# Norms of the latent projections placed among the matmuls, value weights released in halves, and another slot order for layer 1's first expert loads

## The chip, the cores and the metric

The kernel runs on one core of one Trainium2 chip. TensorE multiplies, ScalarE (ACT) and VectorE (DVE) work elementwise, GpSimd (POOL) helps with a few elementwise products, and SyncE (SP) issues the DMAs that bring weights from HBM. The engines run side by side and meet only at semaphores. The metric is the device time of one launch in microseconds (us).

## The reference

`reference` runs two blocks in sequence on x (512 tokens x 1024 channels). `first_block` has two layers. Each layer projects both the 512 tokens and 256 context tokens, does two kinds of attention and a short convolution, merges the branches, and then runs an expert layer in which each of 16 experts takes its best tokens. `second_block` is one layer more, with a dilated attention and a latent attention whose input is normalised twice before it is expanded. What matters here of the latter:

```python
proj = xn @ w_in
q_c  = proj[..., IN_A:IN_A + 512]           # four column tiles of 128
kv_c = proj[..., IN_A + 512:IN_A + 768]     # two column tiles
k_pe = proj[..., IN_A + 768:IN_A + 800]
q  = rms_norm(q_c, q_norm) @ w_uq           # 8 heads x 96, rotary on the last 32
kv = rms_norm(kv_c, kv_norm) @ w_ukv        # 8 heads x (64 key + 64 value)
```

## The kernel before, in words

Activations lie transposed in SBUF, channels on partitions and tokens along the row. The order of all work is written out by hand, one function for each engine and stage (`pe_second`, `act_second`, `dve_second` for the second block), and each engine runs its own list strictly in that order. A `Signal` counts finished steps; `up` raises it, `at` names the count to wait for.

**Dense products in three passes.** float32 accuracy comes from splitting each operand into a high and a low part in a reduced format. For a weight piece of up to 128 x 1024 values that SP has loaded into one of six half slots of `ring`, ScalarE copies the high part to WH (`act_high`, L538), VectorE subtracts to get the low part WL (`dve_low`, L547), and TensorE multiplies (`pe_linear3`, L574). WH and WL hold two pieces, so piece q may be split only when TensorE has finished with piece q-2, and `act_high` waits for the `dn` signal of the *unit* (one call of a product) to which that piece belongs. All units have one piece, except the value units ("v" of each layer, and three of them in the second block), which have two of 512 rows each. `pe_values3` (L593) multiplies them with tokens as the output rows, steps k=0..3 from the first piece and k=4..7 from the second.

**PSUM.** Four tiles go round in a fixed queue: `bank.take(key, freed)` gives the next tile and notes what frees it for the one after.

**Latent projections.** In the second block, after the dilated attention (AD), six units ("c",0) to ("c",5) give q_c and kv_c, a unit "pe" gives k_pe. ScalarE copies each result out (L2295). Then `act_norm` squares the tiles (L694), TensorE sums the squares over partitions with a matrix of ones (L711), ScalarE makes the reciprocal root by Ln and Exp (L729, L731; two table loads), and VectorE multiplies (`dve_norm`, L2383). This is done for "nq" (4 tiles), then for "nkv" (2 tiles). `act_aside` (L602) and `dve_aside` (L607) split the four normalised q tiles into high and low parts. Then come eight heads of queries, ("uq", h//2), two heads for each weight piece (`pe_aside`, L622), each followed by its rotary (`pe_rope` L873, `act_rope_in` L880, POOL L894, DVE L901 and L910), then keys and values from KV by plain float32 products (L2213, L2220), and the latent attention (AM).

**Expert loads.** Layer 1's 192 loads of 1 MB go through SP in the order in which TensorE uses them (`sp_experts`, L2559). There are 12 slots: 0 to 2 are `ring`, 3 to 6 lie in memory freed once the layer's norm sum is done (`p_n`, L723), 7 to 11 lie in the arena and are used once. Of the latter, 7 to 9 are free when h2 is transposed (L1494) and 10 and 11 when the mask is transposed (L1504). Load n < 12 goes to slot n; after that the seven slots 0 to 6 go round, and a load waits until the one before it in its slot has been multiplied (L1899 for gate and up, L1934 for down):

```python
s = self.n if self.n < len(self.aps) else (self.n - len(self.aps)) % self.turn
```

The functions that the diff touches follow.

Of the kernel before, what the change touches and what calls it, by code (L numbers as in the profile page):

```python
# [14 lines left out]
NX = 512  # L15
# [192 lines left out]
class Slots:  # L208

    def __init__(self, aps, sems, once=0):
        self.aps, self.sems, self.count, self.n, self.turn = aps, sems, [0] * len(sems), 0, len(aps) - once

    def add(self, srcs, many, kind, what):
        s = self.n if self.n < len(self.aps) else (self.n - len(self.aps)) % self.turn
        self.n += 1
        self.count[s] += 16 * len(srcs)
        return s, srcs, many, kind, what, (self.sems[s], self.count[s])
# [16 lines left out]
def build(nc, I, cst, cmask, crope, at, out):  # L236
    ctx = ExitStack()
    with ctx:
# [94 lines left out]

        MD, ME, MO = [None] * 3, [None] * 2, [None] * 2
        ONCE = (14336, 16384, 22528, 18432, 20480)
        fulls = [ring[:, i * SLOT:(i + 1) * SLOT] for i in range(KEPT)]
        early = []
        for l in (0, 1):
# [9 lines left out]
            MO[l].stack.close()  # L348
            under.close()
        MD[2] = dense_memory(2)  # L350
        ES = [Slots(fulls + early[0] + MO[0].slots, s_w), Slots(fulls + early[1] + [AR(a, SLOT) for a in ONCE], s_w[:7] + s_o, len(ONCE))]

        identb = MB[:, MI:MI + 128]
        ident = K("ident")
# [169 lines left out]
        def unit_of_split(X, q):  # L524
            return next(u for u, x in enumerate(X.units) if x[0] <= q < x[1])

        def act_high(e, X, u):
            if u >= len(X.units):  # L530
                return
            m = MD[int(X.key[1])]
            for q, (s, srcs, many, kind, what, arrived) in split_pieces(X, u):
                e.wait_ge(*arrived)
                if q > 1:
                    e.wait_ge(*dn.at(X.key, unit_of_split(X, q - 2)))
                o = 1024 * (q % 2)
                e.activation(m.WH[:, o:o + many], halves.aps[s][:, 0:many], ACT.Copy).then_inc(*hi.up(X.key, q))  # L538

# [37 lines left out]
        def pe_values3(e, X, name, chunks, low, key, *freed):  # L577
            u = X.unit[name]
            m = MD[int(X.key[1])]
            wh, wl = halves_of(X, u)  # L580
            bufs = []
            for n in range(0, chunks, 4):
                ps, when = bank.take((key, n // 4), freed[n // 4])
                bufs.append(ps)
                for w in when:
                    e.wait_ge(*w)
            e.wait_ge(*lo.at(X.key, X.units[u][1] - 1))
            for k in range(KD):
                if low:
                    e.wait_ge(*low(k))  # L590
                for c in range(chunks):
                    for p, (h, w) in enumerate(((m.XH, wh), (m.XL, wh), (m.XH, wl))):
                        i = e.matmul(bufs[c // 4][:, 256 * (c % 4):256 * (c % 4) + 256], h[:, k, c * 128:(c + 1) * 128], w[:, k, :],  # L593
                                     start=k == 0 and p == 0 and c % 2 == 0, stop=k == 7 and p == 2, skip_group_check=True)
            i.then_inc(*dn.up(X.key, u))

        def aside(t, c):
# [1580 lines left out]
        def pe_second(e):  # L2178
# [8 lines left out]
            e.wait_ge(*c_ev.at("x2", "v", 2))  # L2187
            e.wait_ge(*d_o.at("ra", 11))
            pe_attention(e, AD)
            for c in range(6):  # L2190
                pe_linear3(e, X2, ("c", c), 128, NX, ("x2", "c", c), c_ev.at("x2", "c", c))
            pe_linear3(e, X2, "pe", 96, NX, ("rp", "r", 0), c_ev.at("rp", "y", 0))
            pe_rope(e, "rp", 0, NX, 96, ROT[:, 128:256], False)
            for stage, kn in (("nq", 4), ("nkv", 2)):
                pe_norm_take(e, stage)
                for k in range(kn):
                    pe_square(e, stage, k, kn, NX, sqr[k % 2])
            for h in range(8):
                pe_aside(e, X2, ("uq", h // 2), "qc", 96, 4, 96 * (h % 2), h % 2, ("ru", "r", h), c_ev.at("ru", "y", h))
                if h:  # L2200
                    pe_rope(e, "ru", h - 1, NX, 96, ROT[:, 128:256], False)
            pe_rope(e, "ru", 7, NX, 96, ROT[:, 128:256], False)
            p = [X2.plain["ukv", k] for k in (0, 1)]
            for k in (0, 1):
# [68 lines left out]
        def act_norm(e, stage, src, kn, n):  # L2273
            for k in range(kn):
                act_square(e, stage, k, src(k), NX, sqr)
            act_rstd(e, stage, kn, NX, n)

        def act_second(e):
            act_split_gain(e, "gain")
# [8 lines left out]
            e.wait_ge(*d_o.at("ra", 11))  # L2288
            act_attention(e, AD)
            for c in range(6):  # L2290
                act_high(e, X2, X2.unit["c", c] + 1)
                e.wait_ge(*dn.at("x2", X2.unit["c", c]))
                if c == 0:
                    e.wait_ge(*a_pv.at("ad", len(AD.groups) - 1))
                e.activation((QC[:, c, :] if c < 4 else KV[:, c - 4, :]), bank.of["x2", "c", c][:, 0:NX], ACT.Copy).then_inc(*c_ev.up("x2", "c", c))  # L2295
            act_high(e, X2, X2.unit["pe"] + 1)
            act_rope_in(e, "rp", 0, NX, 96, 1.0, dn.at("x2", X2.unit["pe"]), False)
            e.wait_ge(*d_o.at("rp", 0))
            act_norm(e, "nq", lambda k: QC[:, k, :], 4, 512)
            e.wait_ge(*d_an.at("nq", 3))  # L2300
            act_norm(e, "nkv", lambda k: KV[:, k, :], 2, 256)
            e.wait_ge(*d_an.at("nkv", 1))
            for c in range(4):
                act_aside(e, X2, "qc", QC, c)
            for h in range(8):
                if h % 2 == 0:
                    act_high(e, X2, X2.unit["uq", h // 2] + 1)
                act_rope_in(e, "ru", h, NX, 96, 1.0, uq(h), False)
            for h in range(8):
                e.wait_ge(*p_br.at("x2", "kh", h))  # L2310
                e.activation(KH[0:64, h, :], bank.of["x2", "kh", h][0:64, 0:NX], ACT.Copy).then_inc(*c_ev.up("x2", "kh", h))
                e.activation(KH[64:96, h, :], KP[64:96, 0, :], ACT.Copy).then_inc(*c_ev.up("x2", "kp", h))
# [90 lines left out]
        def dve_second(e):  # L2403
# [11 lines left out]
            dve_attention(e, AD)  # L2415
            for c in range(6):
                dve_low(e, X2, X2.unit["c", c] + 1)
            dve_low(e, X2, X2.unit["pe"] + 1)
            dve_rope(e, "rp", 0, NX, 96, rope[:, 3], KP[64:96, 0, :], 64, False)
            dve_norm(e, "nq", QC, 4, 64)  # L2420
            dve_norm(e, "nkv", KV, 2, 68)
            for c in range(4):
                dve_aside(e, X2, "qc", QC, c)
            for h in range(8):
# [225 lines left out]
```

## Time and profile before

| | us |
|---|---|
| median of 3 runs (3680.44 to 3684.14) | 3680.85 |
| profiled execution, its own time | 3679.47 |
| its span, first to last instruction | 3677.7 |
| TensorE busy | 3401.4 (92% of the span) |
| VectorE busy | 1248.5 (34%) |
| ScalarE busy | 1025.4 (28%) |
| GpSimd busy | 186.8 (5%) |
| bytes read from HBM | 595.56 MB, 163 GB/s over the span |
| mean granted TensorE clock | 0.974 |

Times inside the profile count from the first instruction. The rows below give a start and a duration, the engine, the line of the kernel, what is written and read, and in brackets how long the engine had been idle and who ended that. A granted clock of 1.00 is 2.4 GHz and 0.50 is 1.2 GHz; values between are mixtures over a stretch.

### The profile page before, as it was taken

How to read it: one execution, taken by the hardware profiler on the slowest of the kernel's cores; microseconds unless marked ns; L12 is line 12 of the kernel's file. 1: busy time of each engine (PE TensorE's matmuls, PEld its weight loads, DVE VectorE, ACT ScalarE, POOL GpSimd, SP SyncE). 2: the span in 40 equal slices, each digit the busy share in tenths (PEclk: the TensorE clock that was granted, in tenths of full speed). 3: DMA queues.
4: the chain of work that ended last, by engine and by line, in shares of the span. 5: the costliest groups of instructions: out<-in, count | busy, mean ns of one | idle time of the engine just before them, and what ended most of it. 6: DMA issues, size and time to landing. Idle time of an engine off the chain costs nothing.

```text
span 3677.7 us, 48715 instructions
## 1 busy us (share of the span) xinstructions
PE 3401.4 (92%) x21634; PEld 2284.5 (62%) x21634; DVE 1248.5 (34%) x1750; ACT 1025.4 (28%) x1641; POOL 186.8 (5%) x121
## 2 busy tenths in 40 slices
PE   6999999999899999999999979988888989989997
PEld 5787677887534344377668864332247656858886
DVE  3225642323411011144663351111142434453333
ACT  3623532223210000055452231000031344342222
POOL 0100000111100000000000120000001010110000
PEclk9999999999899999999999989999989989989998
DMA  6440014223499989812003348999952111323331
GB/s 223 132 132 24 1 58 115 63 64 128 167 374 354 384 348 358 309 46 81 18 7 98 92 154 313 409 409 409 409 188 69 39 35 41 91 58 97 92 98 46
DMA packets 359985, 600.82 MB, mean 163 GB/s; under 512 B 48770, under 2 KB 242656, under 8 KB 359648
## 3 DMA queue, kind: packets, MB, share of 16 engines
q1 hardware_dynamic: 357024, 596.62, 45.8%
q8 instruction: 171, 2.80, 0.3%
q10 hardware_dynamic: 2752, 1.09, 0.1%
q14 instruction: 38, 0.31, 0.0%
HBM read 595.56 MB, written 2.10 MB: 163 GB/s over the span
## 4 chain that ended last, share of the span: by engine, by line
PE 84%; DMA 6%; DVE 6%; ACT 3%; issue 1%; ACTq 0%; POOL 0%; POOLq 0%; SPq 0%; DVEq 0%
PE ps L574 32%; PE ps L1904 6%; PE ps L2256 5%; PE ps L1060 4%; PE ps L622 4%; PE ps L1899 3%; PE ps L1149 3%; PE ps L1907 3%; PE ps L1938 3%; PE ps L1110 3%; PE ps L1324 3%; DMA ring<-in_w_e_down 3%; DMA ring<-in_w_e_up 2%; PE ps L593 2%; PE ps L1934 2%; PE ps L1551 2%
## 5 line engine op out<-in xcount | busy, mean ns | idle before, releaser
L574 PE MATMUL ps<-xh,wh 128*128 128x512 f32 x1912 | 650.9, 378 | 35.8 <-DVE xl L2118 11.4
L574 PE MATMUL ps<-xl,wh 128*128 128x512 f32 x1912 | 632.9, 369 | 0.0
L574 PE MATMUL ps<-xh,wl 128*128 128x512 f32 x1912 | 632.7, 369 | 0.0
L547 DVE TENSOR_TENSOR wl<-ring,wh 128x1024 fp32r<-128x1024 f32 (+1 forms) x259 | 333.8, 1290 | 615.2 <-ACT wh L538 613.9
L574 PEld LDWEIGHTS ps<-xh,wh 128*128 128x128 f32 x1912 | 332.7, 190 | 123.1 <-issue 39.3
L538 ACT ACTIVATE wh<-ring 128x1024 fp32r<-128x1024 f32 (+1 forms) x259 | 271.7, 1050 | 457.2 <-PE ps L574 168.1
L574 PEld LDWEIGHTS ps<-xl,wh 128*128 128x128 f32 x1912 | 332.9, 191 | 63.5 <-issue 4.3
L574 PEld LDWEIGHTS ps<-xh,wl 128*128 128x128 f32 x1912 | 331.5, 190 | 62.0
L1904 PE MATMUL ps<-ring,arena 128*32 128x512 f32 x2048 | 267.2, 593 | 1.0 <-DVE arena L1686 1.0
L1899 PE MATMUL ps<-ring,arena 128*64 128x512 f32 x984 | 226.9, 599 | 17.9 <-DMA ring<-in_w_e_gate 9.0
L1899 PEld LDWEIGHTS ps<-ring,arena 128*64 128x64 f32 x984 | 66.4, 136 | 154.7 <-issue 101.4
L1907 PEld LDWEIGHTS ps<-ring,arena 128*32 128x32 f32 x2048 | 66.7, 110 | 153.0 <-issue 153.0
L1907 PE MATMUL ps<-ring,arena 128*32 128x256 f32 x2048 | 157.4, 379 | 0.0
L1071 DVE TENSOR_REDUCE sm<-ps 128x2 f32<-128x1536 f32 (+3 forms) x96 | 142.3, 1482 | 43.6 <-PE ps L1060 43.5
L1060 PE MATMUL ps<-arena 64*128 64x256 f32 (+3 forms) x800 | 150.2, 449 | 2.6 <-DVE arena L1020 1.8
L1110 PE MATMUL ps<-consts,tmp 128*128 128x128 f32 x832 | 127.3, 285 | 20.0 <-DVE arena L1166 12.0
L1089 ACT ACTIVATE tmp<-ps,sm 128x768 f32<-128x768 f32 (+3 forms) x176 | 132.7, 762 | 46.3 <-DVE sm L1074 38.8
L1934 PE MATMUL ps<-ring,arena 128*64 128x512 f32 x512 | 114.6, 595 | 31.5 <-DMA ring<-in_w_e_down 23.9
L1110 PEld LDWEIGHTS ps<-consts,tmp 128*128 128x128 f32 x832 | 88.8, 141 | 58.4 <-issue 21.6
L2059 DVE SCALAR_TENSOR_TENSOR y<-ps,gate,y 128x1024 fp32r<-128x1024 f32 x16 | 20.5, 1284 | 307.0 <-ACT y L1994 307.0
L1938 PE MATMUL ps<-ring,hbuf 128*32 128x512 f32 x1024 | 121.8, 592 | 0.8 <-DVE hbuf L2051 0.8
L1149 PE MATMUL ps<-arena 128*64 128x256 f32 (+1 forms) x896 | 99.6, 368 | 14.6 <-DVE arena L1133 14.6
(271 smaller groups left out, 4376.7 us busy)
## 6 DMA issues: line engine op xcount, KB each, us to landing
ring<-in_w_e_down SPq DMA_DIRECT2D x128, 1024.0 KB, 8.2
ring<-in_w_e_gate SPq DMA_DIRECT2D x126, 1024.0 KB, 9.0
ring<-in_w_e_up SPq DMA_DIRECT2D x125, 1024.0 KB, 9.1
ring<-in_w_in SPq DMA_DIRECT2D x116, 512.0 KB, 3.9
ring<-in_w_ada SPq DMA_DIRECT2D x96, 512.0 KB, 4.7
ring<-in_w_ff SPq DMA_DIRECT2D x64, 512.0 KB, 3.9
ring<-in_w_out SPq DMA_DIRECT2D x24, 512.0 KB, 3.7
ring<-in_w_in SPq DMA_DIRECT2D x40, 256.0 KB, 3.8
```

What stands on the lines that cost most here:

```text
L538: e.activation(m.WH[:, o:o + many], halves.aps[s][:, 0:many], ACT.Copy).then_inc(*hi.up(X.key, q))
L547: e.tensor_tensor(m.WL[:, o:o + many], halves.aps[s][:, 0:many], m.WH[:, o:o + many].bitcast(F32), ALU.subtract).then_inc(*lo.up(X.key, q))
L574: i = e.matmul(ps[0:M, a:b], w[:, k, 0:M], h[:, k, a:b], start=k == 0 and p == 0, stop=k == 7 and p == 2)
L1060: x = e.matmul(ps[:, col:col + k.shape[-1]], q, k, start=first, stop=last, skip_group_check=True)
L1110: x = e.transpose(ps[:, 128 * c:128 * c + 128], src[:, u, 128 * b:128 * b + 128], ident)
L1149: e.matmul(ps[r0:r0 + 64, q0:q1], v, pt, start=x == 0, stop=x == len(pv) - 1, skip_group_check=True)
L1899: i = e.matmul(pa[64 * h:64 * h + 64, 512 * w:512 * w + 512], rows_of(1, kk, x, 0, 64), W[:, k, 512 * h:512 * h + 512], start=kk == 0, sto ...
L1904: e.matmul(pa[64 * h + g:64 * h + g + 32, 512 * w:512 * w + 512], rows_of(0, kk, x, g, g + 32), W[:, k, 512 * h:512 * h + 512], start=kk = ...
L1907: i = e.matmul(pb[32 * q:32 * q + 32, 256 * w:256 * w + 256], rows_of(0, kk, x, 64, 96), W[:, k, 256 * q:256 * q + 256], start=kk == 0 and ...
L1934: i = e.matmul(ps[64 * x:64 * x + 64, 512 * h:512 * h + 512], HT2[p % 2][:, x, k % 4, k // 4, :], w, start=k == 0, stop=k == 7)
L1938: e.matmul(ps[64 * x + g:64 * x + g + 32, 512 * h:512 * h + 512], HX[:, k, 64 * x + g:64 * x + g + 32], w, start=k == 0, stop=k == 7, skip ...
L2256: i = e.matmul(accs(d), w[:, 0, d * 128:(d + 1) * 128], h[:, f % 8, 0:NX], start=f == 0 and p == 0, stop=f == 31 and p == 2)
```

## The change

It has three parts.

**Value units in halves.** `pe_values3` waits for the low part of its first piece before k=0 and of its second before k=4, where it waited for the second before k=0. It raises a second signal, `dn(..., "half")`, after k=3, and `act_high` waits for that instead of the whole unit when the piece it overwrites is the first of two (`multiplied`).

**Norms among the projections.** TensorE sums the "nq" squares after unit ("c",4), and the "nkv" squares after the first rotary of the heads. ScalarE squares the q tiles after copying out ("c",3), makes the root after ("c",4), splits the q tiles before the rotary of "pe", and makes the "nkv" root after head 1. VectorE follows. The squares get buffers of their own (`sqm`).

**Slot order.** The first twelve loads of layer 1 go to slots 0, 1, 2, 7, 3, 8, 4, 9, 5, 10, 6, 11.

```diff
+            return dn.at(X.key, u, "half") if q < X.units[u][1] - 1 else dn.at(X.key, u)
...
-                    e.wait_ge(*dn.at(X.key, unit_of_split(X, q - 2)))
+                    e.wait_ge(*multiplied(X, q - 2))
...
-            e.wait_ge(*lo.at(X.key, X.units[u][1] - 1))
+            first = X.units[u][0]
             for k in range(KD):
+                if k % 4 == 0:
+                    e.wait_ge(*lo.at(X.key, first + k // 4))
...
+                if k == 3:
+                    i.then_inc(*dn.up(X.key, u, "half"))
...
-        s = self.n if self.n < len(self.aps) else (self.n - len(self.aps)) % self.turn
+        s = self.first[self.n] if self.n < len(self.aps) else (self.n - len(self.aps)) % self.turn
...
+        FIRST = (0, 1, 2, 7, 3, 8, 4, 9, 5, 10, 6, 11)
...
 pe_second
+            def norm(stage, kn):
+                pe_norm_take(e, stage)
+                for k in range(kn):
+                    pe_square(e, stage, k, kn, NX, sqm[k % 2])
             for c in range(6):
                 pe_linear3(e, X2, ("c", c), 128, NX, ("x2", "c", c), c_ev.at("x2", "c", c))
+                if c == 4:
+                    norm("nq", 4)
...
-            for stage, kn in (("nq", 4), ("nkv", 2)):
-                pe_norm_take(e, stage)
-                for k in range(kn):
-                    pe_square(e, stage, k, kn, NX, sqr[k % 2])
...
+                if h == 1:
+                    norm("nkv", 2)
...
 act_second
+                if c == 3:
+                    act_high(e, X2, X2.unit["c", 4] + 1)
+                    for k in range(4):
+                        e.wait_ge(*c_ev.at("x2", "c", k))
+                        act_square(e, "nq", k, QC[:, k, :], NX, sqm)
+                if c == 4:
+                    act_high(e, X2, X2.unit["c", 5] + 1)
+                    act_rstd(e, "nq", 4, NX, 512)
             act_high(e, X2, X2.unit["pe"] + 1)
+            for c in range(4):
+                e.wait_ge(*d_an.at("nq", c))
+                act_aside(e, X2, "qc", QC, c)
+            for k in range(2):
+                e.wait_ge(*c_ev.at("x2", "c", 4 + k))
+                act_square(e, "nkv", k, KV[:, k, :], NX, sqm)
             act_rope_in(e, "rp", 0, NX, 96, 1.0, dn.at("x2", X2.unit["pe"]), False)
             e.wait_ge(*d_o.at("rp", 0))
-            act_norm(e, "nq", lambda k: QC[:, k, :], 4, 512)
-            e.wait_ge(*d_an.at("nq", 3))
-            act_norm(e, "nkv", lambda k: KV[:, k, :], 2, 256)
-            e.wait_ge(*d_an.at("nkv", 1))
...
                 act_rope_in(e, "ru", h, NX, 96, 1.0, uq(h), False)
+                if h == 1:
+                    act_rstd(e, "nkv", 2, NX, 256)
...
 dve_second
+            dve_norm(e, "nq", QC, 4, 64)
             dve_low(e, X2, X2.unit["pe"] + 1)
...
+                if h == 3:
+                    dve_norm(e, "nkv", KV, 2, 68)
```

## Rows read from the trace of the kernel before

**Rows 1.** The page: the chain that ended last by engine, and a costly group.

```profile
PE 84%; DMA 6%; DVE 6%; ACT 3%; issue 1%; ACTq 0%; POOL 0%; POOLq 0%; SPq 0%; DVEq 0%
...
L538 ACT ACTIVATE wh<-ring 128x1024 fp32r<-128x1024 f32 (+1 forms) x259 | 271.7, 1050 | 457.2 <-PE ps L574 168.1
```

**Rows 2.** Chain in order of time, value units: start us, us, what.

```profile
54.55 18.83 PE ps L593 x144
75.83 8.59 PE ps L574 x48
...
1589.27 19.38 PE ps L593 x144
1611.19 18.18 PE ps L574 x96
...
2805.38 11.76 PE ps L593 x96
2820.72 11.78 PE ps L593 x96
2836.18 13.16 PE ps L593 x96
```

**Rows 3.** TensorE timeline: the last rotary ahead of the value units.

```profile
2803.63 1.13 PE L873 MATMUL ps<-tmp 128*128 128x512 f32 x2 [0.83 <-ACT tmp L880]
```

**Rows 4.** Chain in order of time, latent projections and heads.

```profile
2899.03 38.44 PE ps L574 x168
...
2963.11 8.59 PE ps L622 x48
2972.57 2.80 PE ps L622 x24
```

**Rows 5.** Stretches: length, busy by engine, granted clock, DMA share, GB/s.

```profile
2837.00:2850.00 13.00, 12.33 (x94) 12.12 (x93) 0.00 (x0) 0.57 (x1) 0.00 (x0) 0.91 0.24 67
2938.00:2963.00 25.00, 10.21 (x14) 3.37 (x14) 6.24 (x10) 12.79 (x18) 1.26 (x1) 0.71 0.00 0
2963.00:2971.00 8.00, 7.88 (x44) 7.92 (x45) 2.64 (x4) 2.13 (x4) 0.00 (x0) 0.62 0.26 68
2971.00:2996.00 25.00, 25.00 (x167) 20.11 (x166) 11.81 (x16) 6.57 (x10) 8.93 (x7) 1.00 0.17 43
```

**Rows 6.** ScalarE timeline, latent norms.

```profile
2945.63 0.63 ACT L694 ACTIVATE tmp<-arena 128x512 f32<-128x512 f32 x1 [0.81 <-PE ps L711]
...
2961.61 2.19 ACT L602 ACTIVATE xh<-arena 128x512 fp32r<-128x512 f32 x4 [1.48 <-DVE arena L2383]
2963.71 0.82 ACT L538 ACTIVATE wh<-ring 128x768 fp32r<-128x768 f32 x1
```

**Rows 7.** VectorE timeline, latent norms.

```profile
2940.68 0.68 DVE L910 TENSOR_TENSOR arena<-tmp 32x512 f32<-32x512 f32 x1 [0.66 <-POOL tmp L894]
2950.23 2.74 DVE L2383 SCALAR_TENSOR_TENSOR arena<-arena,PT,tmp 128x512 f32<-128x512 f32 x4 [8.87 <-ACT tmp L731]
...
2962.28 2.50 DVE L607 TENSOR_TENSOR xl<-arena,xh 128x512 fp32r<-128x512 f32 x4 [0.70 <-ACT xh L602]
```

**Rows 8.** TensorE timeline: one sum of squares in layer 1, and the rotary of "pe".

```profile
2168.12 1.02 PE L720 MATMUL ps<-tmp,ones 128*128 128x512 f32 x2
...
2938.23 1.07 PE L873 MATMUL ps<-tmp 96*96 96x512 f32 x2 [0.78 <-ACT tmp L880]
```

**Rows 9.** SP timeline, layer 1: issue of loads 3, 7, 18 and 19.

```profile
2170.94 0.37 SPq L2559 DMA_DIRECT2D ring<-in_w_e_up  x1
...
2190.18 0.37 SPq L2559 DMA_DIRECT2D arena<-in_w_e_up  x1
...
2231.14 0.37 SPq L2559 DMA_DIRECT2D ring<-in_w_e_gate  x1
...
2244.03 0.37 SPq L2559 DMA_DIRECT2D ring<-in_w_e_up  x1
```

**Rows 10.** DMA, 2236 to 2256 us, forty slices of 0.5 us.

```profile
GB/s 410 410 172 115 57 25 0 0 0 0 0 0 0 0 0 0 0 0 33 156 434 393 418 426 410 377 410 434 410 410 418 418 442 410 352 287 360 385 352 303
```

More of the change, by code:

```diff
@@ L208, with __init__ @@
 class Slots:
-    def __init__(self, aps, sems, once=0):
+    def __init__(self, aps, sems, once=0, first=None):
         self.aps, self.sems, self.count, self.n, self.turn = aps, sems, [0] * len(sems), 0, len(aps) - once
+        self.first = first or range(len(aps))
     def add(self, srcs, many, kind, what):
-        s = self.n if self.n < len(self.aps) else (self.n - len(self.aps)) % self.turn
+        s = self.first[self.n] if self.n < len(self.aps) else (self.n - len(self.aps)) % self.turn
         self.n += 1
@@ L350, in build @@
         MD[2] = dense_memory(2)
-        ES = [Slots(fulls + early[0] + MO[0].slots, s_w), Slots(fulls + early[1] + [AR(a, SLOT) for a in ONCE], s_w[:7] + s_o, len(ONCE))]
+        ES = [Slots(fulls + early[0] + MO[0].slots, s_w), Slots(fulls + early[1] + [AR(a, SLOT) for a in ONCE], s_w[:7] + s_o, len(ONCE), FIRST)]
         identb = MB[:, MI:MI + 128]
@@ L525, in unit_of_split, with multiplied @@
             return next(u for u, x in enumerate(X.units) if x[0] <= q < x[1])
+        def multiplied(X, q):
+            u = unit_of_split(X, q)
+            return dn.at(X.key, u, "half") if q < X.units[u][1] - 1 else dn.at(X.key, u)
         def act_high(e, X, u):
@@ L2271, in accs @@
             return bank.of["acc", (d // 2 + 1) % 4][:, 512 * (d % 2):512 * (d % 2) + 512]
[L2273 to L2276, printed above, removed]
+        sqm = [tmp[:, 4096:4608], tmp[:, 4608:5120]]
         def act_second(e):
@@ L2290, in act_second @@
             for c in range(6):
-                act_high(e, X2, X2.unit["c", c] + 1)
+                if c < 4:
+                    act_high(e, X2, X2.unit["c", c] + 1)
                 e.wait_ge(*dn.at("x2", X2.unit["c", c]))
@@ L2295, in act_second @@
                 e.activation((QC[:, c, :] if c < 4 else KV[:, c - 4, :]), bank.of["x2", "c", c][:, 0:NX], ACT.Copy).then_inc(*c_ev.up("x2", "c", c))
-            act_high(e, X2, X2.unit["pe"] + 1)
+                if c == 3:
[6 more added lines that the diff above has]
+                    act_rstd(e, "nq", 4, NX, 512)
+            act_high(e, X2, X2.unit["pe"] + 1)
+            for c in range(4):
[4 more added lines that the diff above has]
+                act_square(e, "nkv", k, KV[:, k, :], NX, sqm)
             act_rope_in(e, "rp", 0, NX, 96, 1.0, dn.at("x2", X2.unit["pe"]), False)
             e.wait_ge(*d_o.at("rp", 0))
-            act_norm(e, "nq", lambda k: QC[:, k, :], 4, 512)
-            e.wait_ge(*d_an.at("nq", 3))
-            act_norm(e, "nkv", lambda k: KV[:, k, :], 2, 256)
-            e.wait_ge(*d_an.at("nkv", 1))
-            for c in range(4):
-                act_aside(e, X2, "qc", QC, c)
             for h in range(8):
@@ L2417, in dve_second @@
                 dve_low(e, X2, X2.unit["c", c] + 1)
+            dve_norm(e, "nq", QC, 4, 64)
             dve_low(e, X2, X2.unit["pe"] + 1)
-            dve_rope(e, "rp", 0, NX, 96, rope[:, 3], KP[64:96, 0, :], 64, False)
-            dve_norm(e, "nq", QC, 4, 64)
-            dve_norm(e, "nkv", KV, 2, 68)
             for c in range(4):
                 dve_aside(e, X2, "qc", QC, c)
+            dve_rope(e, "rp", 0, NX, 96, rope[:, 3], KP[64:96, 0, :], 64, False)
             for h in range(8):
```

## The prediction, made before the changed kernel was run

> **What bounds the kernel now.** I read the page first, then the chain in order of time, then each engine's timeline around the three places that the diff touches, then stretches with their granted clock. TensorE carries 84% of the chain that ended last [rows 1]; in the dense stages the whole path is its own list, and a microsecond without a multiplication there is a microsecond of the run. The exception is layer 1's expert stage, where loads arrive at some 410 GB/s without a break [rows 10]. Each edit is therefore priced as a hole in TensorE's list, or as bytes moved earlier.
>
> The holes in the chain: after each value unit TensorE stands still until the next unit's pieces are split [rows 2], and between the end of "pe" and the first head lie 25.6 us (2899.03 + 38.44 = 2937.5 to 2963.11) with little but the norms [rows 4]. After long holes the granted clock is low: 0.71 and 0.62 behind the norms, 0.91 in the third value unit, against 1.00 once the heads run [rows 5].
>
> **Value units in halves.** ScalarE can split the piece behind a value unit at its middle. The mid-point lies some 5.9 us (layers: 9.5 us) ahead of the unit's end, and splitting one piece takes 1.05 us on ScalarE [rows 1] and a little more on VectorE, so it is ready. The second piece of the next unit still waits for the end, but is wanted only after four steps, 5.9 us later. So each hole closes:
> - Layer 0: 75.83 - (54.55 + 18.83) = 2.45 us [rows 2].
> - Layer 1: 1611.19 - (1589.27 + 19.38) = 2.54 us [rows 2]. The two units behind it take 18.18 us, against 2 x 8.59 = 17.2 in layer 0: 1.0 more at the lower clock, which I count as regained.
> - Second block: ahead of the first unit TensorE waits for the low part of the second piece, from the end of the last rotary (2803.63 + 1.13 = 2804.76) to 2805.38, 0.6 us [rows 2, 3]. Between the units 2820.72 - 2817.14 = 3.58 and 2836.18 - 2832.50 = 3.68. The third unit takes 13.16, not 11.77: 1.4 at the lower clock. Behind it ScalarE now splits the next piece (1.05) before it copies the values out, and attention waits for that copy; with the split done at the half, 1.0 is gained.
>
> Both layers' gains pass on: behind them come stages led by TensorE, and layer 1's load stream starts only when TensorE has multiplied load 12, so it moves with it. Sum: 2.45 + 3.54 + 10.26 = 16.3 us. The added waits stand in front of work whose inputs are long there, and no instruction is added. The start of the layers' value units stays: what they wait for there is the split of the activations.
>
> **Norms among the projections.** One dense unit takes 38.44 / 7 = 5.49 us [rows 4], so ("c",4) ends at 2899.03 + 5 x 5.49 = 2926.5, and the first head starts 36.6 us later. Count the new list from that end (time 0). *TensorE:* four sums of squares at the 1.02 us of layer 1's [rows 8], to 4.1; ("c",5) to 9.6; "pe" to 15.1; the rotary starts 0.8 later as now and takes 1.0 [rows 8], to 16.9; then head 0. *ScalarE* did two squares ahead, does the other two between TensorE's sums by about 2.8 (0.63 each [rows 6]), copies ("c",4) out to 3.4, splits "pe" to 4.3 (0.82), and makes the root. A root takes, from the last square's end (2946.26) to VectorE's first product at 2950.23 [rows 6, 7], 4.0 us with both table loads: 8.3. It copies ("c",5) at its end, to 10.2, splits the first head piece to 11.0, and the q tiles to 13.2 (2.19 [rows 6]). *VectorE* normalises from 8.3 to 11.1 (2.74), and finishes the low parts of the tiles at about 14.5 (2.50 and one weight piece [rows 7]). TensorE wants them at 16.9: 2.4 us of slack. The hole shrinks by 36.6 - 16.9 = 19.7.
>
> Queued behind the new waits: behind ScalarE's third square stand the copy of ("c",4) and the split of "pe", wanted only at 9.6; behind the rotary of "pe" (done 3.5 us after its end at most, [rows 7, 8]: 2940.68 + 0.68 against 2937.5 is 3.9) stand the next split and head 0's copy, wanted by TensorE only after head 1, 7.5 us after "pe". At head 1 the "nkv" root holds ScalarE for some 5 us, and behind it are the split of the third head piece, wanted two heads later (7 us), and head 2's copy, wanted 8 us later. VectorE's two more products (1.4) lie between rotaries that leave it idle more than half the time. I find nobody waiting. The two "nkv" sums now cost TensorE 2 x 1.02 = 2.0 between heads; they were in the old hole.
>
> The heads: the first two take 8.59, later ones 2.80 to 2.87 each [rows 4], so 2.9 us were lost to the low clock. With no hole over 1 us before them I count that as gained. Sum: 19.7 - 2.0 + 2.9 = 20.6 us. The squares and the weighted sum themselves are unchanged in number.
>
> Rows show both levels: 0.62 granted over the first heads, 1.00 after [rows 5]. The Trainium skill, "TensorE: Matmul & The Clock Gate", Part 1, says that the clock is halved after idling and released by sustained activity; by that rule all three clock terms (5.3 us) come back. Without it the sum would be 31.6 instead of 36.9. The switch of table costs 1.3 us in the trace (the root starts that long after the square). "ScalarE: Activation LUTs", What ACT_TABLE_LOAD costs, in the Trainium skill, gives 2.66 us for a switch, with a drain behind the load; two switches would be 2.8 us longer and would use up the slack of 2.4. The measured root has no room for such drains, so I keep the row.
>
> **Slot order.** Load 3 now waits for h2 instead of the norm sum: 2190.18 instead of 2170.94, and loads 4 to 6 stand behind it in SP's queue [rows 9]. They still land long before their turn: load 6 was multiplied when load 18 could go out, at 2231.14, and six loads at 410 GB/s take 15.4 us from 2190. Loads 15 to 18 then wait for loads 4, 6, 8 and 10 instead of 3 to 6, so the stream is spread out, the last leaving when load 10 is done, about 2239.7 if loads 6 to 12 are evenly spaced, instead of 2231.14. But load 19 waits for load 12 before and after (2244.03). Nineteen loads have gone out at that time either way, and from there the stream runs without a break to the end of the stage. The trace shows the DMA engines idle from 2239 to 2245 [rows 10]: the new order fills that hole with bytes which it takes from earlier holes. Bounds: a gain of 6 us if it filled it with new bytes, a loss of 19.2 if the late start weighed in full. By the count of loads I take 0.
>
> **Sum.** 16.3 + 20.6 + 0 = 36.9 us. The profiled execution took 3679.47 (span 3677.7) and would take 3642.6; the median of the runs, 3680.85, lies 1.4 above it: **3644**.
>
> **Rivals.**
> - *The low clock stays.* The holes close, but the three clock terms are not regained: 3649. For it, 0.91 was granted over a stretch in which TensorE was busy 12.33 of 13 us [rows 5]; against it, 1.00 in the heads.
> - *A queue stalls.* The root in the heads, or the late split of the q tiles, holds up TensorE. The slack is 2.4 us and the root 4: a price of 2 to 6 us, 3646 to 3650. By the page's price for table switches it would be near the lower end, about 3645.
> - *The slot order matters.* It gains the 6 us of the idle stretch, 3638, or loses 19, 3663. The count of loads speaks against both.
> - *Slower.* Layer 1's loads lose their overlap: if the new order left one load in flight at a time through the stage, each would add at least the 1.2 us from issue (2244.03) to the first bytes (2245.2) [rows 9, 10]. This decides from about 31 such loads on (36.9 / 1.2); all 173 left would cost 208 us, 3852 in all. Against it: from load 12 on the seven slots go round as before, and only seven loads change what they wait for.
> - *No change.* The holes move instead of closing, ScalarE being so late in all of them: 3681. Its busy 12.8 of 25 us in the norm stretch [rows 5] speaks against it.
>
> **How the numbers follow.** Forecast 0.62, low clock 0.12, a stall 0.12, slot gain 0.04, slot loss 0.05, no change 0.02, slower by overlap lost 0.03. The range 3637 to 3652 takes in the forecast, the low clock, the stalls and the slot gain, 0.90, less what their own sizes may miss. A measurement of this kernel can tell about 0.2% (7 us) from no change: faster 0.95, same 0.02, slower 0.03.
>
> **What would show it.** Right: the chain has no hole over 1 us behind a value unit; the third takes 11.8; the first head starts about 17 us after ("c",4) ends, and two heads take 5.7; load 19 leaves when load 12 is done, and layer 1's stage is as long as before. Wrong: TensorE waiting for `xl` or `wl` at the heads, for ScalarE's squares behind ("c",4), or for a load in layer 1's first experts.

## The result, and the profile after

| | before | after |
|---|---|---|
| median of the runs, us | 3681.49 (4 runs, 3680.44 to 3684.14) | 3639.64 (4 runs, 3637.78 to 3642.18) |
| ratio, 95% interval | | 0.9886 [0.9869, 0.9903] |
| span of the profiled execution, us | 3677.7 | 3640.3 |
| mean granted TensorE clock | 0.974 | 0.977 |

The change saves 41.9 us (1.14%); 36.9 were forecast. The two profiled spans lie only 37.4 us apart, as the forecast had it: the profiled execution of after, at 3642.18 us, was the slowest of its four, 2.5 us above their median, and the one of before, at 3679.47, lies 2.0 us below its own. These 4.5 us of the gain are the difference between executions and cannot be found between these two profiles.

The page of after, the chain by engine, answers to [rows 1]:

```profile
span 3640.3 us, 48719 instructions
...
PE 85%; DMA 6%; DVE 5%; ACT 3%; issue 1%; ACTq 0%; POOL 0%; POOLq 0%; SPq 0%; DVEq 0%
```

The chain of after in order of time (start us, us, what); L581 is `pe_linear3` now, L602 `pe_values3`, L633 `pe_aside`, L722 `pe_square`:

```profile
55.08 20.12 PE ps L602 x144
75.20 8.48 PE ps L581 x48
...
1589.18 19.46 PE ps L602 x144
1608.64 16.97 PE ps L581 x96
...
2802.56 34.56 PE ps L602 x288
...
2885.79 27.44 PE ps L581 x120
2913.22 3.62 PE ps L722 x8
2916.85 11.02 PE ps L581 x48
...
2929.70 5.67 PE ps L633 x48
...
2937.95 2.79 PE ps L633 x24
```

Read it against [rows 2, 4]. Every value unit ends where the next link starts: 1589.18 + 19.46 = 1608.64, with no hole. In the second block the three value units have become one link, 34.56 us for 288 matmuls, where three links of 11.76, 11.78 and 13.16 us lay with 3.6 and 3.7 us between them; in after that link starts where the rotary ahead of it ends (2801.43 + 1.13 = 2802.56), so the hole of 0.6 us there is closed too. Behind ("c",4) the chain now goes to the sums of squares (3.62), then ("c",5) and "pe" (11.02), and the first head starts 43.9 us after ("c",0), where it took 64.1, and 16.5 us after ("c",4) ends (2913.22 to 2929.70; 16.9 were forecast). Two heads take 5.67 us, which is two times a later head.

Stretches at the start of the values of layer 0, before and after, and over the first heads of after (length, busy time by engine, granted clock, DMA share, GB/s). The last answers to the 0.62 of [rows 5]:

```profile
54.00:60.00 6.00, 5.45 (x34) 5.48 (x35) 5.89 (x13) 2.65 (x6) 0.00 (x0) 0.71 0.65 154
...
54.00:60.00 6.00, 4.92 (x23) 4.95 (x24) 5.89 (x11) 2.88 (x6) 0.00 (x0) 0.50 0.71 197
...
2928.00:2936.00 8.00, 7.37 (x52) 6.43 (x53) 2.33 (x3) 2.40 (x4) 1.30 (x1) 1.00 0.14 31
```

The heads ran at full clock. Layer 0's value unit began at half clock in both executions; in this one the clock stayed low for longer (0.50 up to 60 us, where before had 0.71), and the unit took 20.12 us instead of 18.83. The hole behind it is closed all the same (55.08 + 20.12 = 75.20).

ScalarE and VectorE of after around the norm, which answer to [rows 6, 7]: the two table loads with Ln and Exp, and the split of the q tiles.

```profile
2916.90 1.28 ACT L740 ACT_TABLE_LOAD   x1
2918.20 0.69 ACT L740 ACTIVATE tmp<-ps,eps 128x512 f32<-128x512 f32 x1
2918.90 1.28 ACT L742 ACT_TABLE_LOAD   x1
2920.20 0.63 ACT L742 ACTIVATE tmp<-tmp 128x512 f32<-128x512 f32 x1
```

```profile
2924.57 2.49 DVE L618 TENSOR_TENSOR xl<-arena,xh 128x512 fp32r<-128x512 f32 x4
```

The last low part is done at 2924.57 + 2.49 = 2927.06, and the first head's first matmul is recorded at 2929.13 while its link in the chain starts at 2929.70: a slack of 2.1 to 2.6 us around the forecast 2.4. Ahead of that, TensorE and its sums in after's timeline answer to [rows 8]:

```profile
2913.06 3.78 PE L722 MATMUL ps<-tmp,ones 128*128 128x512 f32 x8
...
2928.63 1.07 PE L884 MATMUL ps<-tmp 96*96 96x512 f32 x2 [0.77 <-ACT tmp L891]
```

SP of after issues loads 3, 18 and 19 at these times ([rows 9] had 2170.94, 2231.14, 2244.03):

```profile
2186.80 0.37 SPq L2584 DMA_DIRECT2D arena<-in_w_e_up  x1
...
2235.94 0.37 SPq L2584 DMA_DIRECT2D ring<-in_w_e_gate  x1
2240.66 0.37 SPq L2584 DMA_DIRECT2D ring<-in_w_e_up  x1
```

Load 3 goes out later and the stream is spread, as forecast. The first expert matmul stands at 2210.8 in after and at 2214.2 before, and load 19 leaves 29.9 us behind it in both (2240.66 - 2210.8 and 2244.03 - 2214.2).

### The profile page after: what moved, and what is told of

Same layout as the page of the kernel before. It is cut to its first block, busy times and chain, and to the rows that moved or that the text cites. A ratio compares the mean times of both kernels' runs of the same rounds, so it can differ in the third digit from the quotient of the medians.

```text
span 3640.3 us, 48719 instructions
## 1 busy us (share of the span) xinstructions
PE 3396.2 (93%) x21630; PEld 2280.0 (63%) x21634; DVE 1246.9 (34%) x1750; ACT 1025.2 (28%) x1641; POOL 187.7 (5%) x121
## 3 DMA queue, kind: packets, MB, share of 16 engines
q1 hardware_dynamic: 357024, 596.62, 46.3%
## 4 chain that ended last, share of the span: by engine, by line
PE 85%; DMA 6%; DVE 5%; ACT 3%; issue 1%; ACTq 0%; POOL 0%; POOLq 0%; SPq 0%; DVEq 0%
PE ps L581 32%; PE ps L1915 6%; PE ps L2272 5%; PE ps L1071 4%; PE ps L1910 4%; PE ps L633 3%; PE ps L1160 3%; PE ps L1918 3%; PE ps L1949 3%; PE ps L1121 3%; PE ps L1335 3%; DMA ring<-in_w_e_up 3%; DMA ring<-in_w_e_down 2%; PE ps L602 2%; PE ps L1945 2%; PE ps L1840 2%
## 5 line engine op out<-in xcount | busy, mean ns | idle before, releaser
L581 PE MATMUL ps<-xh,wh 128*128 128x512 f32 x1912 | 648.0, 377 | 32.6 <-DVE xl L2129 13.8
L581 PE MATMUL ps<-xl,wh 128*128 128x512 f32 x1912 | 632.2, 369 | 0.0
L581 PE MATMUL ps<-xh,wl 128*128 128x512 f32 x1912 | 631.9, 369 | 0.0
L581 PEld LDWEIGHTS ps<-xh,wh 128*128 128x128 f32 x1912 | 330.8, 189 | 120.1 <-issue 37.8
L581 PEld LDWEIGHTS ps<-xl,wh 128*128 128x128 f32 x1912 | 331.1, 190 | 63.3 <-issue 4.5
L581 PEld LDWEIGHTS ps<-xh,wl 128*128 128x128 f32 x1912 | 330.9, 190 | 62.4
L1121 PE MATMUL ps<-consts,tmp 128*128 128x128 f32 x832 | 128.6, 287 | 19.6 <-DVE arena L1177 12.0
```

The lines of the kernel that those rows point to most:

```text
L581: i = e.matmul(ps[0:M, a:b], w[:, k, 0:M], h[:, k, a:b], start=k == 0 and p == 0, stop=k == 7 and p == 2)
L1121: x = e.transpose(ps[:, 128 * c:128 * c + 128], src[:, u, 128 * b:128 * b + 128], ident)
```

## The experiments

Beside each result stands the time of the kernel before, measured together with it, and the ratio with its 95% interval. Each kernel was profiled once.

### One part at a time

`e1_values` keeps only the value units in halves: `multiplied`, the waits by piece and the "half" signal.

```diff
             for k in range(KD):
+                if k % 4 == 0:
+                    e.wait_ge(*lo.at(X.key, first + k // 4))
```

> Only the value units in halves; norms and slot order as before. My theory: the three places give 2.5 + 3.5 + 10.3 = 16.3 us, so about 3665. Rival one (the lower clock behind the holes is not caused by them): 13.9 us, the third value unit still takes over 13. Rival two (the layers' share is absorbed before the expert stages): only the second block's 10.3 us, 3671. The profile decides between them: the start of layer 1's first expert, and the length of the third value unit in the second block (11.8 by my theory).

Measured: 3662.72 us against 3681.33, ratio 0.9944 [0.9931, 0.9956], so -18.6. In its chain the three value units of the second block are one link of 34.56 us, three times 11.5, so the third is back at full speed. Layer 1's first expert starts at 2206.9 instead of 2214.2, 7.3 us earlier, of which 1.0 is an earlier start of layer 0's values. The layers' gain is passed on and not absorbed.

```profile
2797.26 34.56 PE ps L600 x288
```

`e2_norms` keeps only the norms among the projections (the hunks of `pe_second`, `act_second` and `dve_second`).

> Only the norms among the projections; value units and slot order as before. My theory: 20.6 us, about 3661; the first head starts 17 us after the unit (c,4) ends, and the first two heads take 5.7 us. Rival (clock not regained): 17.7 us, the first two heads take 8.6. Rival (a queue stalls): a hole in TensorE's list inside the heads, 2 to 6 us less.

Measured: 3660.14 against 3681.33, ratio 0.994 [0.9928, 0.9953], so -21.2. Its chain has what this part leaves alone, the unit behind layer 0's values and the second block's second value unit, and its own two heads:

```profile
76.66 10.28 PE ps L574 x48
...
2823.22 13.27 PE ps L593 x96
...
2947.04 5.67 PE ps L622 x48
```

The second value unit takes 13.27 us here and took 11.78 in [rows 2], and the first unit behind layer 0's values takes 10.28 instead of 8.59. No edit touches them, and the holes ahead of them are the old ones. The granted clock over the second value unit, in before and then in `e2_norms` (length, busy time by engine, clock, DMA share, GB/s), tells the two apart:

```profile
2820.70:2832.50 11.80, 11.77 (x96) 11.56 (x96) 0.00 (x0) 0.00 (x0) 0.00 (x0) 1.00 0.32 90
...
2823.20:2836.50 13.30, 13.26 (x96) 13.06 (x96) 0.00 (x0) 0.00 (x0) 0.00 (x0) 0.87 0.30 79
```

The same five places in all the profiles that still have some of the old holes (us; a dash where the kernel has closed or filled the hole):

| | unit behind layer 0's values | second value unit, second block | its first value unit to ("c",0) | first two heads | last product |
|---|---|---|---|---|---|
| before | 8.59 | 11.78 | 93.65 | 8.59 | 175.99 |
| `e3_slots` | 8.59 | 13.27 | 96.75 | 8.61 | 175.94 |
| `e8_seven_slots` | 10.16 | 13.27 | 95.21 | 7.83 | 174.37 |
| `e5_busy_hole` | 10.16 | 13.27 | 95.22 | - | 174.36 |
| `e2_norms` | 10.28 | 13.27 | 95.22 | - | 174.38 |
| `e6_second_only` | 8.59 | - | - | 7.33 | 174.34 |
| `e1_values` | - | - | - | 7.74 | 174.37 |

The price of a hole in clock thus varies from execution to execution. The profile of before was cheap in the first three columns and dear in the last two.

`e3_slots` keeps only the slot order.

```diff
-        s = self.n if self.n < len(self.aps) else (self.n - len(self.aps)) % self.turn
+        s = self.first[self.n] if self.n < len(self.aps) else (self.n - len(self.aps)) % self.turn
```

> Only the other slot order for layer 1's first twelve loads. My theory: 0 us, 3681, since load 19 waits for load 12 either way; layer 1's expert stage from first to last multiplication is as long as before (468.5 to 471 us). Rival (it explains what the whole change gained beyond my 36.9 us): a gain of 3 to 6 us, load 19 leaving earlier after the first expert's start than before. Rival (the late start weighs): a loss of 1 to 19 us.

Measured: 3683.33 against 3681.33, ratio 1.0002 [0.9993, 1.0011]. The view by source line gives the first and last time of the gate and up matmuls (L1899, L1901) and of the down matmuls (L1934, L1936). Before:

```profile
L1899 PE MATMUL ps<-ring,arena x984: 592/592/644, 2214.2 to 2673.4; 128*64 128x512 f32 x197
L1934 PE MATMUL ps<-ring,arena x512: 592/592/643, 2270.9 to 2696.0; 128*64 128x512 f32 x171
```

`e3_slots`:

```profile
L1901 PE MATMUL ps<-ring,arena x984: 592/592/644, 2214.6 to 2674.7; 128*64 128x512 f32 x197
L1936 PE MATMUL ps<-ring,arena x512: 592/592/644, 2271.3 to 2697.4; 128*64 128x512 f32 x171
```

The stage takes 2696.0 - 2214.2 = 481.8 us before and 2697.4 - 2214.6 = 482.8 with the new order: nothing gained. (The 468.5 to 471 us of the expectation end at the start of the last down product, 2682.66 before.) In all twelve profiles that have the twelve slots, with either order, the stage takes 481.8 to 483.3 us.

`e4_no_slots` is the whole change without the slot order.

```diff
-        ES = [Slots(fulls + early[0] + MO[0].slots, s_w), Slots(fulls + early[1] + [AR(a, SLOT) for a in ONCE], s_w[:7] + s_o, len(ONCE), FIRST)]
+        ES = [Slots(fulls + early[0] + MO[0].slots, s_w), Slots(fulls + early[1] + [AR(a, SLOT) for a in ONCE], s_w[:7] + s_o, len(ONCE))]
```

> The whole change without the slot order. My theory: the same time as the whole change, 3640 within 2 us, and the sum of the two parts alone. Rival (slot order gains 3 to 6 us): 3643 to 3646.

Measured: 3639.51 against 3681.33, ratio 0.9883 [0.9869, 0.9896], and again 3639.51, 0.9883 [0.9866, 0.9899], when it ran once more (`e4_again`) beside later kernels. After has 0.9886. The order of the slots is worth nothing that can be measured, and the parts add up: 18.6 + 21.2 = 39.8 of 41.9 by the medians.

> The whole change without the slot order once more, to stand beside the two kernels below. 3638 to 3641.

### Is it idling that costs the clock?

`e5_busy_hole` is the kernel before, with useless matmuls in the norm hole. They read parts of WH and XH that nobody writes then, and their result is never read. Every sum and every wait of the norms stays; one wait is added ahead, for the low part of the first head piece.

```diff
+            e.wait_ge(*lo.at("x2", X2.units[X2.unit["uq", 0]][0]))
             for stage, kn in (("nq", 4), ("nkv", 2)):
                 pe_norm_take(e, stage)
+                idle(bank.of["norm", stage], 8 if stage == "nq" else 32)
...
+            if name == ("uq", 0) and o == 0:
+                for _ in range(28):
+                    e.matmul(ps[:, 0:256], m.WH[:, 1024:1152], m.XH[:, 0, 0:256], start=True, stop=True)
```

> The kernel before, with 8, 32 and 28 matmuls of no use (128 x 256, into banks that the next product overwrites) in the three parts of the norm hole in which TensorE waits. They end before the work that it waits for arrives. My theory (idling lowered the clock behind the hole): the hole is as long as before, but the first two heads take 5.7 instead of 8.6 us, so the run is 2 to 3 us shorter although TensorE does more. Rival (the lower clock there has another cause): 8.6 us as before.

TensorE of `e5_busy_hole`, two groups of the added matmuls, its chain from ("c",0) to the first heads, and the stretch of these heads:

```profile
2955.28 4.39 PE L2199 MATMUL ps<-xh,wh 128*128 128x256 f32 x32
...
2963.43 3.91 PE L620 MATMUL ps<-xh,wh 128*128 128x256 f32 x28
```

```profile
2907.38 38.45 PE ps L574 x168
...
2969.55 5.90 PE ps L625 x48
...
2969.50:2975.50 6.00, 5.95 (x49) 5.91 (x50) 2.67 (x4) 2.17 (x5) 0.00 (x0) 1.00 0.35 87
```

With a hole that is still there in the chain (62.2 us from ("c",0) to the first head, 64.1 before) the two heads take 5.90 us at a granted 1.00. The five profiles with an idle hole have 7.33 to 8.61, so this one lies outside what the same hole gives by chance. The low clock over the heads comes from what TensorE did in the hole, and not from the heads' own work. The total, 3681.15 in a single run, says nothing about it, since the first expert of layer 1 stood 5.6 us later than in the profile of before, through stages that no edit touches.

`e7_sums_late` is the whole change with the "nq" sums one unit later, which opens a hole again.

```diff
-                if c == 4:
+                if c == 5:
                     norm("nq", 4)
```

> The whole change, but TensorE makes the nq sums after the unit (c,5) instead of (c,4); ScalarE and VectorE keep their lists. My accounting: ScalarE now stands at the third square until (c,5) ends, the split of pe behind it comes 1.5 us too late for TensorE, and the split q tiles 1.9 us too late for the first head; the stretch from the start of (c,0) to the first head is 3.4 us longer than the 43.9 of the whole change, 47.3. Rival (the slack of 2.4 us was larger than I counted): below 45.

Its chain, ("c",0) to ("c",5) and the first heads:

```profile
2884.30 32.88 PE ps L581 x144
...
2930.95 7.22 PE ps L633 x48
```

From ("c",0) to the first head it is 46.65 us, against 43.9 in after, where 47.3 was expected. TensorE now waits for the root's chain ahead of the rotary of "pe":

```profile
2921.97 0.44 PE L581 MATMUL ps<-xh,wh 128*96 128x512 f32 x1 [1.18 <-DVE wl L554]
...
2929.88 1.07 PE L884 MATMUL ps<-tmp 96*96 96x512 f32 x2 [2.14 <-ACT tmp L891]
```

Behind holes of 1.18 and 2.14 us the two heads take 7.22 us, 1.5 more than in after. Its single run took 3645.08 us, 5.4 more than after's median. The two units that the change puts between the sums and the rotary just cover the root; one is too few.

### Where the halves gain

`e6_second_only` is `e1_values` with the halves in the second block alone.

```diff
+            return dn.at(X.key, u, "half") if q < X.units[u][1] - 1 and X.key == "x2" else dn.at(X.key, u)
...
+                    e.wait_ge(*lo.at(X.key, first + (k // 4 if X.key == "x2" else 1)))
```

> Value units in halves in the second block only; layers 0 and 1, norms and slots as before. My theory: the second block's share of 10.3 us, about 3671, which leaves the layers 6 to 8 us of the 18.6 that the part gave alone. Rival (the layers' share is absorbed before the expert stages): 3663 to 3665, the same as with all three places.

Measured: 3667.53 against 3681.37, ratio 0.9966 [0.9954, 0.9978], so -13.8, where 10.3 were forecast. The three value units are one link again:

```profile
2805.17 34.56 PE ps L600 x288
```

The two layers' share by the medians is the rest, 18.6 - 13.8 = 4.8 us. The six runs of this kernel lie between 3664.3 and 3674.3, and its interval reaches from 8.1 to 16.9 us saved, so these two numbers are known to a few microseconds only. The traces divide the gain otherwise. From the start of layer 0's values to its first expert the six kernels with the old hole take 944.5 to 949.5 us (mean 946.2), and the five with the halves and an unchanged start 942.3 to 944.7 (943.2). From the start of layer 1's values to its first expert it is 624.9 to 625.9 (625.4) and 621.4 to 622.5 (621.9). That makes 6.5 us for the two layers, where 6.0 were forecast.

### What the extra slots do

`e8_seven_slots` is the kernel before without its five slots of one use, so that load 7 already waits for a matmul.

```diff
-        ES = [Slots(fulls + early[0] + MO[0].slots, s_w), Slots(fulls + early[1] + [AR(a, SLOT) for a in ONCE], s_w[:7] + s_o, len(ONCE))]
+        ES = [Slots(fulls + early[0] + MO[0].slots, s_w), Slots(fulls + early[1], s_w[:7])]
```

> The kernel before without its five single-use slots in layer 1: seven slots go round from the start. My theory (what counts is when load 12 is done, since load 19 waits for it with twelve slots or with seven): load 19 again leaves when load 12 is done; the DMA engines then still have some 4 us of earlier loads to carry, less than the 6 us for which they stood idle; so 0 to 3 us slower, 3681 to 3684. Rival (each single-use slot saves the time of its 1 MB in the stream, 2.56 us): 12.8 us slower, 3694.

Measured: 3684.82 against 3681.37, ratio 1.0008 [0.9999, 1.0017], so +3.4; the interval just takes in no change at all. SP's issue of load 19, and the stage's first and last matmuls:

```profile
2243.65 0.37 SPq L2559 DMA_DIRECT2D ring<-in_w_e_up  x1
```

```profile
L1899 PE MATMUL ps<-ring,arena x1024: 592/592/669, 2213.8 to 2677.3; 128*64 128x512 f32 x171
...
L1934 PE MATMUL ps<-ring,arena x512: 592/592/1061, 2270.5 to 2700.0; 128*64 128x512 f32 x171
```

The DMA rate of the same kernel from 2200 to 2280 us, forty slices of 2 us:

```profile
GB/s 0 0 0 0 0 0 0 8 123 414 350 356 412 385 379 412 354 397 408 420 410 412 412 410 410 410 410 410 410 410 410 410 410 410 410 408 414 408 408 410
```

Five megabytes fewer are in place, which at 410 GB/s would be 12.8 us; the stage takes 2700.0 - 2213.8 = 486.2 us, 2.9 to 4.4 more than the 481.8 to 483.3 of all profiles with twelve slots. The stream flows from 2216 on without a break, and load 19 leaves at 2243.65 instead of 2244.03. So most of the time that the five loads would have saved was never there. Before, the DMA engines finish early and stand idle from 2239 to 2245 [rows 10]; without the slots they work through that time.

### Further holes

The chain of `e4_no_slots` in its second run still has holes which the same two means close. `e9_further` moves the rotary of "pe" behind head 0, puts head 1's weight piece ahead of the wait for it, and splits layer 0's second value piece between the activation tiles instead of behind them.

```diff
# act_split_mod, dve_split_mod
+                if l == 0 and k == 1:
+                    act_high(e, X, 0, slice(1, 2))
...
+                if l == 0 and k == 2:
+                    dve_low(e, X, 0, slice(1, 2))
...
# act_second
+            act_high(e, X2, X2.unit["uq", 0] + 1)
             e.wait_ge(*d_o.at("rp", 0))
```

> The whole change without the slot order, and two small holes more: TensorE turns pe only behind the first head (the rotary's input then is long there; 0.8 to 1.0 us), and in layer 0 the second value piece is split behind the second and third tile of activations instead of ahead of them, so that the values start 2.3 us earlier and end 2.1 us earlier. About 3 us less than the kernel beside it, 3636 to 3637. Rival (VectorE is what layer 0's values wait for at the end, and it does the same work): 1 us less only.

Measured: 3637.82 against 3681.91, ratio 0.9879 [0.9864, 0.9893], 1.7 us less than `e4_again`, measured together with it. The start of layer 0's values in the chain of `e4_again`, then of `e9_further`, and ScalarE's split of the second value piece in each:

```profile
54.39 19.82 PE ps L602 x144
...
52.69 19.84 PE ps L602 x144
```

```profile
48.75 1.06 ACT L545 ACTIVATE wh<-ring 128x1024 fp32r<-128x1024 f32 x1 [0.67 <-DMA ring<-in_w_in]
...
52.15 1.04 ACT L545 ACTIVATE wh<-ring 128x1024 fp32r<-128x1024 f32 x1
```

The first piece is split at the same time in both (47.03 and 47.06). In `e4_again` the activation tiles stand behind the second, which waits for its DMA; in `e9_further` they don't. So 1.7 us come from the start of layer 0's values, where 2.3 were expected. The rotary gave its part too: from ("c",0) to the third head `e9_further` takes 0.85 us less (51.35 and 52.20). The two chains differ by 2.5 us at these places, the medians by 1.7, and the intervals overlap, so the total alone would not tell the kernels apart.

`e10_tail` adds this: the second product of the feed-forward layer at the end waits for the last tile of the first to be activated and split. The first three tiles it needs are written into a free part of XH and XL while the first product still runs.

```diff
+                moving = aside(h, f) if f < 3 else h[:, f % 8, 0:NX]
```

> The kernel above, and the first three tiles of the feed-forward's second product split into columns of XH and XL that the first product does not read, so that TensorE does not stand still for 2.2 us between the two. 2.2 us less than the kernel above where the clock did not fall behind that hole, 3.8 where it did (the products took 174.4 or 176.0 us): 3633 to 3634.

The chain of `e4_again` ahead of that product, then of `e10_tail`:

```profile
3427.03 0.61 ACT arena L2378
...
3429.23 10.90 PE ps L2272 x47
```

```profile
3421.24 0.61 ACT arena L2393
...
3422.20 17.93 PE ps L2278 x78
```

One link on ScalarE and a short issue stand where ScalarE, VectorE and VectorE had followed each other; the hole shrinks from 2.2 to 1.0 us, and not to nothing as expected. Measured: 3635.57 against 3681.91, ratio 0.9875 [0.986, 0.989]. This kernel has the lowest median here, 46.3 us below before. Against `e4_again` it is 3.9 us lower (four runs each, 3633.68 to 3638.42 and 3636.24 to 3641.29, which still overlap). Its step beyond `e9_further` is 2.2 us by the medians, the number expected, but the chain shows 1.2 of it; the rest is not shown to be the edit's.

## Why the prediction was right

The forecast was 3644 us, the result 3639.64, within the range. Its steps, in order:

| term | forecast | by the medians | by the stages of all traces |
|---|---|---|---|
| value halves, second block | 10.3 | 13.8 (`e6_second_only`; interval 8.1 to 16.9) | 12.6 |
| value halves, two layers | 6.0 | 4.8 (`e1_values` less `e6_second_only`) | 6.5 |
| norms among the projections | 20.6 | 21.2 (`e2_norms`; interval 17.3 to 26.5) | 20.7 |
| slot order | 0 | 0 (`e3_slots`, `e4_no_slots`) | 0 |
| all | 36.9 | 41.9 (interval 35.7 to 48.2) | 39.8 |

The last column takes means over the profiles with and without each part. For the second block they are 95.2 us (the five numbers of the table above) and 83.2 from the first value unit to ("c",0), and 0.6 for the hole ahead of it. For the norms they are 72.8 from ("c",0) to the third head (73.54, 73.64, 72.54, 72.24 and 72.28 in before, `e3_slots`, `e8_seven_slots`, `e1_values` and `e6_second_only`) and 52.2.

**Value units in halves.** The mechanism held at every unit: 1608.64, 75.20 and the single link of 34.56 us. From the first value unit of the second block to ("c",0) before's profile has 93.65 us, after's 83.2, and `e1_values`, `e4_no_slots` and `e6_second_only` have 83.2 too: 10.4 less, where the forecast for this stretch was 9.7 (10.3 without the 0.6 ahead of it). But the other four profiles that leave this part alone have 95.2 to 96.8, and against the mean of the five the halves gain 12.0. In the layers the hole of layer 1 closed as counted (21.92 us from the start of its values to the next unit, now 19.46), and the two units behind it fell from 18.18 to 16.97. In layer 0 the gain shows only in part in after's profile, because there the clock stayed at 0.50 for longer in the values, which began 0.5 us later.

**The step that was mis-sized** is the clock term: I counted 5.3 us over three places, all from [rows 2, 4], one execution. The other traces show that this execution did not stand for the rest. It had no lowered clock in the second value unit (11.78 us, elsewhere 13.27) nor behind layer 0's values (8.59, in three of six 10.2), so I counted nothing at either; and it had the dearest heads but one (8.59 us, elsewhere 7.33 to 8.61, so 2.9 was near the top of 1.7 to 2.9). Most of what was missing lies in the second block's value units, 12.6 by the traces against 10.3; the layers add 0.5, and in the norms the errors cancel. The last product's 1.6 us, in before and in `e3_slots`, is not an effect of the change, since `e2_norms` has the same hole of 2.2 us ahead of it and 174.38 us. The granted clock over its first 8 us, in before and then in `e2_norms`:

```profile
3467.00:3475.00 8.00, 8.00 (x28) 6.43 (x29) 2.73 (x4) 2.01 (x3) 0.00 (x0) 0.79 0.22 68
...
3450.00:3458.00 8.00, 7.84 (x35) 6.50 (x36) 3.86 (x5) 3.18 (x5) 0.00 (x0) 1.00 0.23 68
```

The traces so account for 39.8 us, 2.9 of the error of 5.0. The remaining 2.1 lie well within the interval of the ratio, 35.7 to 48.2 us saved. The clock at these places is shown in the profiled executions; how often it falls in the others is not known. Unedited stages ahead of layer 1 also move by 2 us or more between executions (the first expert of layer 0 starts at 999.9 before, 999.8 after and 1001.7 in `e2_norms`). That the forecast 36.9 lies so near the 37.4 between the two profiled spans is partly luck, since 1.6 of the latter come from the last product.

**Norms.** The hole went from 64.08 to 43.9 us, measured from ("c",0) to the first head: 20.2, forecast 19.7. The two heads gave 2.92 (forecast 2.9), the four sums took 3.78 (4.1), the two "nkv" sums 1.72 (2.0). Part of this agreement is luck: on the mean of the five profiles with the idle hole the heads gave 2.35 (8.02 less 5.67), and the smaller errors of the hole and the sums made up for it. The slack behind VectorE was about the 2.4 us forecast, and `e7_sums_late` shows that one unit less room costs time. The rivals "a queue stalls" and "the holes move" are refuted by the chain of after, "the low clock stays" by the granted 1.00. `e5_busy_hole` gives the cause, 5.90 with the hole filled against 7.33 to 8.61 without. The Trainium skill, "TensorE: Matmul & The Clock Gate", Part 1, has the clock halved after idling and given back by sustained activity, and here the trace agrees (0.62 behind the idle hole, 1.00 over the same heads in after and in `e5_busy_hole`). From the first head to the end after's profile has 4.0 us less than before's (714.6 and 710.6). The heads less the "nkv" sums make 1.2 and the last product 1.6. The remaining 1.2 lie nearly all between the last matmul of `pe_aside` (L622, later L633) and the last product, 259.6 us before and 258.5 after. The other profiles have 258.6 to 260.1 there, with the norms moved and without, so this is no effect of the change either. Two readings of the prediction were loose. The granted 0.71 of [rows 5] belongs to the norm stretch itself and only the 0.62 to the work behind it; and the rotary of "pe" is done 3.9 us after the unit by the rows it cites, not 3.5 at most, which changes nothing.

**Tables.** The two table loads with Ln and Exp took 3.9 us (2916.90 to 2920.83), each next instruction starting 1.3 us behind the start of its table load. "ScalarE: Activation LUTs", What ACT_TABLE_LOAD costs, in the Trainium skill, states 2.66 us for a switch with its drain; this case doesn't show it, and the measurement decides. By that figure the stall would have been 2.8 - 2.4 = 0.4 us, an estimate that lies below the rival's 2 to 6 us.

**Slot order.** The argument by the count of loads held, and the stage takes 481.8 to 482.8 us in before, after, `e3_slots` and `e4_no_slots`. So the slower rival, 3852 us with the loads' overlap lost, is refuted too. The rivals of a gain of 6 and of a loss of 19 are both refuted: the interval of `e3_slots` reaches from 2.6 us faster to 4.0 slower. `e8_seven_slots` shows why so little hangs on it: the time between the first load and the first wait for a slot is mostly not what ends the stage. What I had bounded there at 0 to 3 us was 3.4, and 2.9 to 4.4 in the stage's own length.

## What to carry to other kernels

When an engine with its own list carries the path, price each edit as a hole in that list, and check two things beside it: when the next operand is ready if it is released at the half, and how late the slowest chain elsewhere (here square, root, product, split) may be before it shows. Two moves of ordinary work made the run 42 us shorter here with no arithmetic added, only waits and signals, and the same reading of what was left found about 4 more by the medians.

Count the clock behind a hole separately, and from several executions. One trace shows only whether the hole lowered the clock that time.

Before reordering prefetches into a stream that is the bound, count loads that have gone out by the time the stream no longer breaks. If that number is the same in both orders, expect little of the order; here it was worth nothing.

## What the runs showed of the hardware

The same hole lowers the clock in some executions and not in others. The 96 matmuls of a value unit behind a hole of 3.6 us took 11.78 us in one profile (granted 1.00) and 13.27 in four others (0.87 in `e2_norms`). The 48 matmuls behind a hole of 2.4 us took 8.59 in three and 10.2 in three. The last product, behind 2.2 us, took 174.37 or 175.99. At these three places a lowered clock cost 1.5 to 1.7 us each time. The outcome behind layer 0's values went with how the values themselves had run: 8.59 us behind the three that took 18.8 to 19.0 us, 10.2 behind the three that took 19.6 to 20.0. Why is not shown. Useless matmuls in a long hole kept the clock up: 5.90 us at 1.00 for the two heads, against 7.33 to 8.61 in five profiles with the hole idle.

Five more megabytes of expert weights loaded ahead of a stage that ran at 410 GB/s saved 2.9 to 4.4 us of it (486.2 in one profile against 481.8 to 483.3 in twelve) and not the 12.8 that their transfer takes.
